# A hand-ordered fp32 transformer kernel: score matrix zeroed on VectorE, gate bounds made one stage earlier, and a new order of the side steps

## What is computed

```
for layer in range(2):                      # first block
    h = rmsnorm(x, norm_mix_g[layer])
    mix = retention_nsa_mixer(h, ...) if layer == 0 else hgrn2_mixer(h, ...)
    x = x + mix
    x = x + swiglu(rmsnorm(x, norm_ffn_g[layer]), w1, w3, w2)
x = rmsnorm(x, final_norm_g)
for l in range(2):                          # second block
    mix = diff_attention(x, ...) if l == 0 else chunk_attention(x, ...)
    x = layer_norm(ALPHA * x + mix, ...)
    x = layer_norm(ALPHA * x + swiglu_2(x, ...), ...)
```

```
lb = jnp.maximum(lb, 0.0)
log_f = jnp.logaddexp(jnp.log(lb), jnp.log1p(-lb) + jax.nn.log_sigmoid(fp))
attn = jnp.sum(qc[:, :, :, None, :] * decay * kc[:, :, None, :, :], axis=-1)
```

## Time and profile before

| | us |
|---|---|
| median of 3 runs | 1330.5 |
| lowest, highest | 1330.25, 1332.86 |
| the profiled execution | 1333.37 |
| its span in the profile | 1331.6 |

### The profile page before, as it was taken

How to read it: one execution, slowest core, us unless ns; L and a number is a source line. 1 busy time by engine, 2 the same in 40 slices (tenths; PEclk the granted TensorE clock), 3 DMA queues, 4 the chain that set the end, 5 groups by cost and what they waited for, 6 DMA issues and landing times.

```text
span 1331.6 us, 19257 instructions
## 1 busy us (share of the span) xinstructions
PE 1301.4 (98%) x7406; PEld 1063.4 (80%) x7406; DVE 394.5 (30%) x813; ACT 717.9 (54%) x1265; POOL 1033.5 (78%) x875
## 2 busy tenths in 40 slices
PE   7999999999989999999999998999999999999997
PEld 5877888888878878888887886888887787788886
DVE  2474311111367452111006545111103343301102
ACT  6656644444678776444435664544444565444531
POOL 7655888888964576888887877788889887788874
PEclk9999999999989999999999999999999999999999
DMA  8532566556642344656665544565656554566652
GB/s 273 157 121 81 170 209 187 180 179 186 188 146 68 116 151 126 206 178 190 188 188 171 169 143 144 187 185 181 190 182 197 192 171 144 161 217 186 194 174 80
DMA packets 63116, 224.90 MB, mean 169 GB/s; under 512 B 7345, under 2 KB 7985, under 8 KB 63025
## 3 DMA queue, kind: packets, MB, share of 16 engines
q1 hardware_dynamic: 62736, 223.57, 55.2%
q10 hardware_dynamic: 288, 0.10, 0.0%
HBM read 222.59 MB, written 1.05 MB: 168 GB/s over the span
## 4 chain that ended last, share of the span: by engine, by line
PE 94%; POOL 2%; ACT 2%; DVE 1%; DMA 1%; issue 0%; SPq 0%; DVEq 0%; ACTq 0%
PE G L1068 28%; PE G L1075 27%; PE G L1069 27%; POOL wlo L2244 2%; PE A L1099 1%; PE A L1173 1%; PE A L1209 1%; PE A L1089 1%; PE G L1173 1%; PE A L1376 1%; ACT whi L1968 1%; PE A L1233 0%; DMA raw<-in_w_e 0%; PE G L1209 0%; PE A L1312 0%
## 5 line engine op out<-in xcount | busy, mean ns | idle before, releaser
L2244 POOL TENSOR_TENSOR wlo<-raw,whi 128x256 fp32r<-128x256 f32 (+1 forms) x867 | 1023.9, 1224 | 280.1 <-ACT whi L1968 279.8
L1968 ACT ACTIVATE whi<-raw 128x1024 fp32r<-128x1024 f32 x403 | 425.5, 1059 | 331.5 <-PE G L1075 319.1
L1068 PE MATMUL G<-whi,xh 128*128 128x512 f32 (+2 forms) x1200 | 463.2, 390 | 11.7 <-DVE xl L1424 8.3
L1069 PE MATMUL G<-whi,xl 128*128 128x512 f32 (+2 forms) x1200 | 450.7, 379 | 0.0
L1075 PE MATMUL G<-wlo,xh 128*128 128x512 f32 (+2 forms) x1200 | 351.5, 379 | 1.1 <-POOL wlo L2244 1.1
L1068 PEld LDWEIGHTS G<-whi,xh 128*128 128x128 f32 x1200 | 227.1, 189 | 55.8 <-issue 13.9
L1069 PEld LDWEIGHTS G<-whi,xl 128*128 128x128 f32 x1200 | 227.4, 190 | 37.9
L1075 PEld LDWEIGHTS G<-wlo,xh 128*128 128x128 f32 x1200 | 218.7, 189 | 46.4 <-POOL wlo L2244 3.3
L1068 PE MATMUL G<-whi,hh 128*128 128x512 f32 x352 | 139.4, 396 | 0.0
L1069 PE MATMUL G<-whi,hl 128*128 128x512 f32 x352 | 138.8, 394 | 0.0
L1075 PE MATMUL G<-wlo,hh 128*128 128x512 f32 x352 | 110.4, 395 | 0.0
(11 more groups left out here) (357 smaller groups left out, 1168.5 us busy)
## 6 DMA issues: line engine op xcount, KB each, us to landing
raw<-in_g SPq DMA_DIRECT2D x88, 512.0 KB, 3.8
raw<-in_u SPq DMA_DIRECT2D x88, 512.0 KB, 4.0
raw<-in_d SPq DMA_DIRECT2D x88, 512.0 KB, 4.2
raw<-in_w_h SPq DMA_DIRECT2D x32, 512.0 KB, 3.6
raw<-in_w_e SPq DMA_DIRECT2D x24, 512.0 KB, 4.2
raw<-in_w_a SPq DMA_DIRECT2D x24, 512.0 KB, 3.7
raw<-in_w_b SPq DMA_DIRECT2D x24, 512.0 KB, 3.8
raw<-in_w_eo SPq DMA_DIRECT2D x8, 512.0 KB, 3.6
```

Of the source, the lines that this page charges most:

```text
L1068: e.matmul(o, sh[:, kt, xs], whi[h][:, ws], start=u.first and j == 0, stop=False)
L1069: e.matmul(o, sl[:, kt, xs], whi[h][:, ws], start=False, stop=False)
L1968: e.activation(whi[c % NH][:, 0:n], raw[c % NR][:, 0:n], ACT.Copy).then_inc(s_hi, 1)
L2244: m = e.tensor_tensor(wlo[c % NH][:, i:j], raw[c % NR][:, i:j], whi[c % NH][:, i:j].bitcast(F), ALU.subtract)
```

## The change

**Code.** (1) `level_scores` loses the matmul of zeros. `decay_heads` (step `H3`) now makes the product that reads columns 0 to 127 of the tile first, then the two others, waits for its own first product, and writes zeros to these columns with a memset on DVE. The tile `ZB` is gone. (2) `B1`, `B2` and `B3` stand in stage 1, behind units 60, 62 and 63, and work in place in `HN`; `B1` takes no tile and no work buffer any more. SP loads their rows at chunk 14 of stage 1, behind a wait for the end of stage 0, in place of chunk 6 of stage 2. (3) `x_turn` of stages 0, 2, 4 and 6 waits also for the last holder of the tile it writes.

```diff
-                if c == first[2] + 6:
-                    e.wait_ge(s_unit, BEGIN[2])
+                if c == first[1] + 14:
+                    e.wait_ge(s_unit, BEGIN[1])
...
+                for k, of in LANE_END.get((st, t), ()) if st >= 0 and st % 2 == 0 else ():
+                    e.wait_ge(S[k], nth(k, *of))
...
-                e.matmul(tile[:, 0:128], ZB[:, :], ZB[:, :], start=True, stop=False, skip_group_check=True)
...
-                _, w = lane_of("B1", key)
...
-                e.memset(ZB[:, :], 0.0)
-                e.tensor_tensor(w[0][:, :], lb, lb, ALU.subtract)
+                e.tensor_tensor(lb, lb, lb, ALU.subtract)
...
-                e.tensor_tensor(w[0][:, 256:1024], tile[:, 256:1024], kq[:, t, 256:1024], ALU.mult)
-                e.tensor_tensor(heads4(w[0][:, 128:256], 2), heads4(tile[:, 128:256], 2),
-                                heads4(kq[:, t, 0:256], 4)[:, 0:4:3, :], ALU.mult)
...
-                m.then_inc(S["H3"], 1)
+                m.then_inc(s_dve, dv.up())
+                e.tensor_tensor(w[0][:, 256:1024], tile[:, 256:1024], kq[:, t, 256:1024], ALU.mult)
+                e.tensor_tensor(heads4(w[0][:, 128:256], 2), heads4(tile[:, 128:256], 2),
+                                heads4(kq[:, t, 0:256], 4)[:, 0:4:3, :], ALU.mult)
+                own()
+                e.memset(tile[:, 0:128], 0.0).then_inc(S["H3"], 1)
```

**Order.** The table is new in all eight stages: the side steps of stages 2, 4 and 6 and the second half of stage 0 stand elsewhere, and so do the steps at the stage changes. Two of its lines:

```diff
-21: T1 0 @0; FD 1; H1 0 0 @1; FE 1; TV 0
+20: EV 2 0; FA 1; T1 0 @2; H1 0 0 @0; TV 0
```

More of the change, by code:

```diff
@@ L254 @@
 -1: -XT 0 0; -SQ 0 0; -XT 1 0; -XH 0 0; HI 0; -XL 0 0; -XH 1 0; HI 1; -XL 1 0
[L255 to L258, removed]
+0: HI 2; -SQ 1 0; -XT 1 1; HI 3
+1: -XH 1 1; -XT 0 1; -RS 0; -XL 1 1
+2: -XH 0 1; -SQ 0 1; -XL 0 1; HI 4
+3: -SQ 1 1
 4: HI 5; -RS 1
@@ L323 @@
 4: SI 0 0
+7: SI 0 1
+12: HM 0 0; HT 0 0
+13: HH 0 0
+14: HL 0 0
+16: HM 0 1; HT 0 1
+17: HH 0 1; HL 0 1
+20: SI 1 0
+23: SI 1 1
+28: HM 1 0; HT 1 0
+29: HH 1 0
+30: HL 1 0
+32: HM 1 1; HT 1 1
+33: HH 1 1; HL 1 1
+36: SI 2 0
+39: SI 2 1
+44: HM 2 0; HT 2 0
+45: HH 2 0
+46: HL 2 0
+48: HM 2 1; HT 2 1
+49: HH 2 1; HL 2 1
+52: SI 3 0
+55: SI 3 1
+60: HM 3 0; B1; HT 3 0
+61: HH 3 0
+62: HL 3 0; B2
+63: B3
+65: HM 3 1
+66: HT 3 1
+67: HH 3 1; HL 3 1
+68: SI 4 0
+71: SI 4 1
+76: HM 4 0; HT 4 0
+77: HH 4 0
@@ new lines @@
+78: HL 4 0
+80: HM 4 1; HT 4 1
+81: HH 4 1; HL 4 1
+82: SI 5 0
+83: SI 5 1
+85: TBL
+86: HM 5 0; HT 5 0
+87: HH 5 0
+88: HL 5 0; HM 5 1; HT 5 1
+89: HH 5 1; HL 5 1
+106: RES 0 0; SQ 0 0; XT 0 0
+110: RES 0 1; SQ 0 1; XT 0 1
+111: XH 0 1; XH 0 0
+112: XL 0 1; XL 0 0
+128: RES 1 0; SQ 1 0; RS 0
+129: XT 1 0; XH 1 0
+""",
+"""
+0: -RES 1 1; -XL 1 0; -XT 1 1
+1: -SQ 1 1; -RS 1
+2: -XH 1 1
+3: -XL 1 1
+4: EV 0 0
+6: EV 0 1
+8: FB 0 @0
+10: FA 0
+12: EV 1 0; FD 0; FE 0
+14: FF 0
+15: FG 0; EV 1 1
+18: FJ 0
@@ new lines @@
+76: XH 0 0; SQ 1 0; XT 1 0; XL 0 0; RS 0; XH 1 0
+78: XL 1 0
+79: RES 0 1
+""",
+"""
+0: -RES 1 1; -XT 1 1; -XT 0 1
+1: -XH 0 1
+2: -XH 1 1; -XL 0 1; -SQ 0 1; -XL 1 1
+3: -SQ 1 1
+4: SI 0 0
+11: -RS 1; SI 0 1
+12: HM 0 0; HT 0 0
+13: HH 0 0
+14: HL 0 0
+16: HM 0 1; HT 0 1
+17: HH 0 1; HL 0 1
+20: SI 1 0
+23: SI 1 1
+28: HM 1 0; HT 1 0
+29: HH 1 0
+30: HL 1 0
+32: HM 1 1; HT 1 1
+33: HH 1 1; HL 1 1
+36: SI 2 0
+39: SI 2 1
+44: HM 2 0; HT 2 0
+45: HH 2 0
+46: HL 2 0
+48: HM 2 1; HT 2 1
+49: HH 2 1; HL 2 1
@@ new lines @@
+52: SI 3 0
+55: SI 3 1
+60: HM 3 0; HT 3 0
+61: HH 3 0
+62: HL 3 0
+64: HM 3 1; HT 3 1
+65: HH 3 1; HL 3 1
+68: SI 4 0
+71: SI 4 1
+76: HM 4 0; HT 4 0
+77: HH 4 0
+78: HL 4 0
+80: HM 4 1; HT 4 1
+81: HH 4 1; HL 4 1
+82: SI 5 0
+83: SI 5 1
+85: TBL
+86: HM 5 0; HT 5 0
+87: HH 5 0
+88: HL 5 0; HM 5 1; HT 5 1
+89: HH 5 1; HL 5 1
+106: RES 0 0; SQ 0 0
+109: SQ 0 1
+110: RES 0 1
+128: RES 1 0; SQ 1 0
+129: RS 0
+130: AP 0 0
+131: AP 1 0; XT 0 0; XH 0 0; RES 1 1; XT 1 0; XL 0 0; SQ 1 1; RS 1; XH 1 0
@@ L544 @@
[L544 to L562 removed]
+106: RES 0 0; BN 0 0
+110: RES 0 1; BN 0 1
@@ new lines @@
+128: RES 1 0; BN 1 0
+129: AG 0; RS 0
+130: AP 0 0; AP 1 0; XT 0 0
+131: XH 0 0; XL 0 0; XT 1 0; RES 1 1
+""",
+"""
+-1: LB 0; LB 1
+0: -BN 1 1; -XH 1 0; -AG 1
+1: -XL 1 0; -RS 1; -AP 0 1
+2: -AP 1 1; -XT 0 1
+3: -XH 0 1; -XL 0 1; -XT 1 1; EV 0 0
+4: TBM 1; -XH 1 1; -XL 1 1
+8: EV 0 1
+9: KT 0 @0
+10: KV 0; KA 0
+11: SC 0 0 @1; EV 1 0
+13: TBM 0
+15: MK 0 0
+17: EV 1 1; EX 0 0
+18: NW 0 0
+19: TR 0 0; EV 2 0
+20: CPA 0 0; AV 0 0
+23: EV 2 1; KA 1
+24: KT 1 @2
+25: KV 1; SC 1 1 @0; WH 0 0
+26: MK 1 1
@@ L563 @@
+3: -XH 0 1; -XL 0 1; -XT 1 1; SI 0 0
+4: -XH 1 1; -XL 1 1
 7: SI 0 1
```

519 lines of the change are left out of this document (180 added, 339 removed).

## The result

| | before | after |
|---|---|---|
| median, us | 1330.93 of 4 | 1323.91 of 4 |
| lowest, highest | 1330.25, 1332.86 | 1322.71, 1325.52 |
| the profiled execution | 1333.37 | 1322.71 |
| its span | 1331.6 | 1320.9 |

The ratio of the medians is 0.9946, with a 95% interval of 0.9928 to 0.9963: 7.0 us or 0.54% less, not the 16.8 us forecast. The two profiled executions lie 10.7 us apart.

The account below looks back on a forecast made before the run. PE, busy 98% of the span, was taken as the bound. Terms -5.4 - 2.4 - 3.9 - 3.7 - 1.6 - 0.7 - 1.5 + 0.4 + 0.3 + 1.7 = -16.8 us gave a median of 1313.7 us, range 1306.5 to 1322.

Parts of the forecast that it names:

- Stage 6: Moved steps at its two changes: -1.6 us from stage 5 to 6, -3.7 us from stage 6 to 7.
- The bounds: `B1` to `B3` moved into stage 1: +0.3 us; at worst, by the shared port, PE waits up to 2.3 us.
- The end: `AP 1 1` and `AP 0 1` swapped, so two of the last four transfers wait for DVE's last one: +0.4 us.
- Stage 2: New order removes three opening waits and the clock's fall, -8.4 us, less 3.0 new waits: -5.4; zeros separately -2.4.
- elsewhere: New orders of stages 0, 4 and 6, with nothing to gain but `ml`: +1.7 us, from 0 to 5.
- right: Signs: stage 2's opening without long waits at full clock, no `ml` wait, `xl` under 3 us, stage 5 starting at full clock.
- wrong: Signs: half clock within stages 2, 4 or 6, memset waits in over four places, an `HT 3 1` wait, PE busy longer.
- the walk: Stage 2's new lists followed: ACT and DVE just behind PE in three places, 1.9 us; 3.0 taken with unseen.
- Stage 4 and its changes: Change from stage 3 to 4 -0.7 us, `ml` wait in stage 4 -1.5, change from stage 4 to 5 -3.9.
- The gain of stage 2 is given back: Rival: stage 2's new order brings back waits and half clock, 8 us, so 1321.7 us; chance 0.2.
- Slower: Rival: the memset delays level scores, about 3 us each; with 7 of 16 places, 1335 us; chance 0.04.
- the order does nothing: Rival: waits only change places, the clock falls as often, only the zeros' 2.4 us stay: 1328 us; chance 0.06.

Follow-up runs that it names:

- the old middle: The kernel after with units 7 to 54 of stage 6 in the order of before, both ends of the stage kept new: 1315.09 us.
- the zeros alone: The kernel before in its own order, with only the 16 matmuls of zeros replaced by DVE's memset: 1327.69 us.
- the late B3: The kernel after with the last gate-bounds step `B3` behind unit 95 of stage 1 instead of unit 63: 1321.12 us.
- the tight opening: The kernel after with stage 2's `H1 0 1`, `H3 0 0` and `H4 0 0` moved up from units 25 and 26 to 22: 1331.19 us.
- the late bias block: The old middle with stage 6's third bias block loaded at unit 30 (from 12) and its POOL step at 33 (from 21): 1319.47 us.

## Why the forecast was wrong

The forecast of 1313.7 us lies 10.2 under the measured 1323.9. 6.1 are the profiled execution (1322.71 against 1316.6), the rest is the step from it to the median. The 6.1 are a sum of larger misses that partly cancel: stage 6 came out 8.1 us worse than its terms, the bounds 2.0 and the end 0.3, while stage 2 came out 2.4 better and the 1.7 for "elsewhere" were set aside for such a miss. That stage 2 made up for a part is luck.

The signs that the prediction named for "right" all came true, but none of them looked at stage 6. Three of those for "wrong" did too: the wait of `HT 3 1` in stage 1, a stretch at half clock within stage 6 (0.50 from 1076 to 1078 us), and PE busy longer at full clock than foreseen, by about 1 us (1295.7 less 1.7 of clock, against 1293).

- **Stage 6** (forecast -5.3 and a share of +1.7; measured +2.77). The step that failed is "I found one place of 0.3 us". I had followed PE, DVE and ACT, and not the chain through SP and POOL: `LB 2` needs a bias buffer that is free only after `MK 0 1`, which the new order puts at unit 30, so load, 8 pieces and `TBM 2` come after it (3.05 us and 1.7 of clock); of these it was the 8 pieces, for with half of them behind `TBM 2` the same late load left a wait of 0.27. Nor did I ask what stands ahead of `EX 0 0`: `TBM 0`, late on POOL, and on ACT a split whose chunk is issued behind 1 MB of layer norm rows (1.23 us together here, 0.56 to 3.59 in other traces of this order). The prediction names no wait of this kind. It also put the new order's own work at nothing, and that came to 1.2 us or more of busy time. The moved steps at the two changes did their part, though less than I said: 4.1 us with the old middle for 5.3, that is 1.35 into stage 6 for 1.6 and 2.7 into stage 7 for 3.7. The waits there were only 1.58 us, and 2.23 + 0.71 us, which should have bounded each term.
- **The bounds** (+0.3, worst +2.3; measured +2.30). The mechanism was on the page and the worst case came true, but by another sum: the first subtraction lost little (it took 1.51 us), the second lost 0.8, and the maximum, which I had counted as not concerned, 2.06.
- **Stage 2** (-5.4 - 2.4; measured -10.24). The waits of 4.08 went, the clock gave back 4.8, and the zeros 2.5 (where the scores come right behind a product, the first of them starts 0.326 us after the start of the last product matmul instead of 0.483). Only 1.15 us of new waits came (0.48 and 0.66), not 3.0: the walk, which had found 1.9, was right to within a microsecond, and the margin for what I had not seen was too large here and missing in stage 6.
- **Stage 4 and its changes** (-3.9 - 0.7 - 1.5): -6.11. Right, and in its parts too: the change from stage 3 to 4 gave 0.5 us for 0.7, the wait for `ml` 1.6 for 1.5, the change to stage 5 4.0 for 3.9. But about 1.3 us of the last are clock that before lost in its profiled execution and that the trace with the zeros alone shows as not lost there; for the median this part was partly luck. Unit 4 of stage 5 starts without a wait, at full clock, as foreseen. Timeline of PE in after, for the earlier trace rows, with the only wait there, 0.48 us for `AP`:

```profile
813.62 0.65 PE L1085 MATMUL A<-CN,X 128*128 128x128 f32 x4 [0.48 <-DVE X L1448]
...
818.48 0.60 PE L1085 MATMUL A<-CN,X 128*128 128x128 f32 x4
...
820.31 0.60 PE L1085 MATMUL A<-CN,X 128*128 128x128 f32 x4
```

- **The end** (+0.4; measured +0.69): the mechanism was right, the size too small.
- **From the profile to the median.** I took 2.9 us off, the distance of before's profiled execution from its median, as if after kept it. But part of the gain in the traces is clock that before loses in some executions only (granted clock 0.993 in the profiled one, 0.997 in the shortest of before, 1327.9 us), while after has its own falls: 0.997 in its profiled execution, 0.994 and 0.995 in the three others. The profiles lie 2.4 above one median and 1.2 under the other. This is 4.1 of the 10.2 us.
- **The rivals.** "The gain of stage 2 is given back" had the right mechanism, waits of 2 us and more and half clock behind them, at the wrong place. Its price of 8 us is near the 8.1 by which stage 6 missed, but that is luck: waits and clock made 5.4 of these, oversized changes and added work the rest. "Slower" through the memset and "the order does nothing" fell.

## To carry to other kernels

Follow every moved step back through the transfer and the helper engine that feed it, to the buffer that must be free first and to what stands ahead of it in the helper's list; an engine list that is shared by a chain and by prefetch work makes the chain wait for late prefetches. Bound each gain by the wait that is there to be gained. And when two kernels lose clock behind waits, compare medians of several executions, not two profiles.

## What the runs showed of the hardware

- A maximum of a 128x1024 tile in SBUF against a constant took 0.69 us with POOL idle and 2.75 beside it: not only instructions with two tensor inputs wait for POOL, and POOL's two pieces beside it and the subtraction got 1.16 us longer in turn.
- The clock after one and the same wait differs between executions: behind 2.09 us in stage 1 it stayed at 1.00 in seven traces and was 0.83 over 10 us in one; behind the 3.05 us in stage 6 it fell in all four traces read, to 0.83 over 10 us in three and to 0.66 in one (the kernel with the late B3). The two waits at the opening of stage 2 cost 4.8 us of clock in the traces of before and of the zeros alone, and 1.7 in that of the tight opening, which is another order of steps. The two kernels without waits over 2 us behind the start-up showed the least spread (1311.51 to 1312.84 in their eight executions); those with such waits spread by 1.4 (the late bias block, four executions) to 8.8 us (the tight opening, ten).
- A chunk of 512 KB issued 0.5 to 1.9 us behind two transfers of layer norm rows of the same size landed 6.0 us behind its issue in after (1025.29 to 1031.33) and 5.3 to 8.3 us in all 13 traces, wherever the rows stood; the page's median for these chunks is 3.7.
